# Gated state mixer: own buffers for the first triangular level, decay products split around the level updates, state values one level up, last turns inside the output tiles

## The reference, cut to what matters

```python
decay = jnp.exp(jnp.where(tril, gc[..., :, None] - gc[..., None, :], -jnp.inf))
k_beta = kc * bc
lmat = jnp.where(strict, jnp.einsum('bhnid,bhnjd->bhnij', k_beta, kc) * decay, 0.0)
rhs = jnp.concatenate([vc * bc, k_beta * jnp.exp(gc)[..., None]], axis=-1)
sol = lax.linalg.triangular_solve(lmat + jnp.eye(c), rhs, left_side=True, lower=True)
u, w = sol[..., :dv], sol[..., dv:]
attn = jnp.where(tril, jnp.einsum('bhnid,bhnjd->bhnij', qc, kc) * decay, 0.0)
...
def step(s, inp):                       # over the chunks, in order
    v_new = u_n - w_n @ s
    o = qd_n @ s + a_n @ v_new
    s = s * cd_n + kt_n.T @ v_new
    return s, o
```

## Time and profile before

| what | value |
|---|---|
| time before, median of 3 runs | 3153.77 us (3151.36 to 3159.57) |
| the profiled execution | 3158.95 us, its span 3157.2 us |
| TensorE busy / VectorE busy / ScalarE busy in the span | 96% / 68% / 50% |
| the stage | about 2046 to 2246 us of the span |

### The profile page before, as it was taken

How to read it: one execution, slowest core, us unless ns; L and a number is a source line. 1 busy time by engine, 2 the same in 40 slices (tenths; PEclk the granted TensorE clock), 3 DMA queues, 4 the chain that set the end, 5 groups by cost and what they waited for, 6 DMA issues and landing times.

```text
span 3157.2 us, 39144 instructions
## 1 busy us (share of the span) xinstructions
PE 3044.5 (96%) x14811; PEld 2349.9 (74%) x14811; DVE 2146.0 (68%) x2336; ACT 1593.9 (50%) x1907; POOL 371.9 (12%) x275
## 2 busy tenths in 40 slices
PE   8999899999999998999999989988999999999998
PEld 7667677777758766677777757877888888788887
DVE  3575888888863377788888865564577646767662
ACT  3573577777753373677777743342312214632211
POOL 0001122222220002122222130110000000000000
PEclk9999999999999999999999999999999999999999
DMA  7203899999962125899999943310232222232322
GB/s 279 109 1 133 300 359 363 357 361 362 362 249 80 37 78 218 318 359 359 362 368 362 358 134 94 74 33 1 94 107 81 94 107 94 88 113 86 101 94 80
DMA packets 174738, 600.50 MB, mean 190 GB/s; under 512 B 25537, under 2 KB 74865, under 8 KB 125203
## 3 DMA queue, kind: packets, MB, share of 16 engines
q1 hardware_dynamic: 140432, 541.22, 48.2%
q0 software_dynamic: 23680, 52.61, 4.7%
q10 hardware_dynamic: 10499, 4.91, 0.6%
HBM read 582.01 MB, written 48.23 MB: 200 GB/s over the span
## 4 chain that ended last, share of the span: by engine, by line
PE 87%; DVE 5%; ACT 3%; DMA 2%; issue 2%; POOL 0%; DVEq 0%; POOLq 0%; ACTq 0%
PE bank L1999 22%; PE bank L2001 22%; PE bank L2000 22%; PE bank L2011 3%; PE bank L2689 2%; PE bank L2389 2%; PE bank L2006 1%; PE bank L2063 1%; PE bank L2064 1%; PE bank L2007 1%; PE bank L2163 1%; PE bank L2430 1%; PE bank L2233 1%; PE bank L2183 1%; DMA ring<-w_gate 1%
## 5 line engine op out<-in xcount | busy, mean ns | idle before, releaser
L2000 PE MATMUL bank<-ring_rounded,big_rounded 128*96 128x512 f32 (+1 forms) x1768 | 695.8, 394 | 0.0
L3441 DVE TENSOR_TENSOR ring_rounded<-ring,big_rounded 128x2048 fp32r<-128x2048 f32 x252 | 572.2, 2289 | 69.8 <-ACT big_rounded L1408 68.5
L1408 ACT ACTIVATE big_rounded<-ring 128x2048 fp32r<-128x2048 f32 x252 | 479.5, 1916 | 69.9 <-DMA ring<-w_up 34.8
L2988 DVE TENSOR_TENSOR ring_rounded<-ring,ring_rounded 128x2048 fp32r<-128x2048 f32 (+2 forms) x118 | 260.3, 2246 | 333.9 <-ACT ring_rounded L1165 333.7
L1165 ACT ACTIVATE ring_rounded<-ring 128x2048 fp32r<-128x2048 f32 (+2 forms) x124 | 226.5, 1876 | 377.1 <-DMA ring<-ffn_w_down 152.7
L1999 PE MATMUL bank<-big_rounded 128*96 128x512 f32 x992 | 396.9, 400 | 9.1 <-DVE XH_rounded L3455 9.1
L2001 PE MATMUL bank<-big_rounded,XH_rounded 128*96 128x512 f32 x992 | 394.2, 397 | 0.0
L2000 PEld LDWEIGHTS bank<-ring_rounded,big_rounded 128*96 128x96 f32 (+1 forms) x1768 | 295.1, 167 | 110.3 <-issue 1.4
L3441 DVE TENSOR_TENSOR ring_rounded<-ring,ring_rounded 128x2048 fp32r<-128x2048 f32 x128 | 292.6, 2288 | 94.4 <-ACT ring_rounded L1408 94.1
L1408 ACT ACTIVATE ring_rounded<-ring 128x2048 fp32r<-128x2048 f32 x128 | 245.0, 1916 | 158.0 <-DMA ring<-w_gate 157.5
L1999 PE MATMUL bank<-ring_rounded,big_rounded 128*96 128x512 f32 (+1 forms) x776 | 309.8, 399 | 1.5 <-DVE big_rounded L4073 0.5
(11 more groups left out here) (486 smaller groups left out, 4844.2 us busy)
## 6 DMA issues: line engine op xcount, KB each, us to landing
ring<-w_up SPq DMA_DIRECT2D x128, 1024.0 KB, 7.7
ring<-w_down SPq DMA_DIRECT2D x128, 1024.0 KB, 6.6
ring<-w_gate SPq DMA_DIRECT2D x128, 1024.0 KB, 8.0
ring<-ffn_w_up SPq DMA_DIRECT2D x44, 1024.0 KB, 6.6
ring<-ret_gdn_w_in SPq DMA_DIRECT2D x8, 2048.0 KB, 12.7
ring<-ffn_w_down SPq DMA_DIRECT2D x8, 2048.0 KB, 7.7
expert_rows<-lnp POOLq DMA_DIRECT2D x1, 12288.0 KB, 40.4
ring<-odd_w_qkv SPq DMA_DIRECT2D x6, 2048.0 KB, 7.9
```

What stands on the lines that cost most here:

```text
L1408: act.activation(one_pass(expert_hi(j)), expert_raw(j), ACT.Copy).then_inc(signal("half_rounded").sem, 1)
L2000: pe.matmul(dst, x_hi, y_lo, start=False, stop=False)
L2988: dve.tensor_tensor(one_pass(w), w, parts(hi(c)[:, ks, :]), ALU.subtract).then_inc(split[c.pair], 1)
L3441: dve.tensor_tensor(one_pass(expert_raw(j)), expert_raw(j), parts(expert_hi(j)), ALU.subtract).then_inc(signal("half_split").sem, 1)
```

## The change

Five edits, all of them of order and of buffers. The number of products, transposes and VectorE instructions stays the same, and so do the transfers.

- ScalarE: `round_chunk` of chunk 7 moves from ahead of the work on chunk 6 to behind `gdn_rows(0)`. VectorE: the remainder of chunk 7 moves behind `gdn_exponents(1)`.
- Level 0 gets own buffers, `G["first"]`, which are the buffers of the mask and of the decay (`gm`, `dec`). Its masking is a function of its own, `first_weights`, and is done right behind `gdn_decayed`, before the end of chunk 7; `gdn_mask(2)` moves behind `first_level((0, 1))`. For the tiles (2, 3) the masking is done at level 4 of (0, 1), and the rest of level 0 stands ahead of `last_level((0, 1))` instead of behind it, in banks 4 and 5.
- `gdn_decayed` is split: `gdn_weighed` (three instructions that free the banks of kk and kq and write `LT`) stands between steps and updates of levels 2 and 4, the other three behind the updates.
- VectorE's `new_values` and `new_state` in the levels of (2, 3) stand one level earlier.
- `turn_y(2)` and `turn_y(3)` run between the halves of output tiles 1 and 2; `rest_of_y(2)` stands ahead of `y_out(3)`.

```diff
+        G["first"] = [G["gm"], G["dec"]]
@@ ScalarE
-                round_chunk(W["mix_in"][7])
                 for t in range(2):
                     keep(N_["GR"], 6, (2 * t,), ACT.Silu)
                     gdn_exps(t)
                     keep(N_["GR"], 6, (2 * t + 1,), ACT.Silu)
                     gdn_rows(t)
+                    if t == 0:
+                        round_chunk(W["mix_in"][7])
@@ TensorE
-                        turn_heads(u, G["T1"][t % 2])
+                        turn_heads(u, G["first"][t % 2])
...
+                first_level((2, 3))
                 last_level((0, 1))
-                first_level((2, 3))
...
-                mix_out(1, lambda: within(3))
-                turn_y(2)
-                mix_out(2)
-                turn_y(3)
+                def last_within():
+                    within(3)
+                    turn_y(2)
+
+                mix_out(1, last_within)
+                mix_out(2, lambda: turn_y(3))
                 mix_out(3)
@@ VectorE
+                def first_weights(ts):
+                    for t in ts:
+                        dve.tensor_tensor(G["first"][t % 2], G["LT"][t], rep(k("level0"), 1, GDN_HEADS), ALU.mult).then_inc(
+                            signal("first_level").sem, 1)
+                        dve.wait_ge(signal("first_level").sem, signal("first_level").next(dve))
...
                 gdn_exponents(0)
                 gdn_mask(1)
-                rest_of_chunk(W["mix_in"][7])
+                gdn_weighed(0)
                 gdn_decayed(0)
                 gdn_exponents(1)
-                gdn_mask(2)
+                rest_of_chunk(W["mix_in"][7])
+                gdn_weighed(1)
                 gdn_decayed(1)
+                first_weights((0, 1))
...
                 first_level((0, 1))
+                gdn_mask(2)
                 rest_of_T("yr_T")
                 for l in range(1, LEVELS - 1):
                     steps(l, (0, 1))
                     if l in (1, 3):
                         gdn_exponents(2 + l // 2)
+                    if l in (2, 4):
+                        gdn_weighed(1 + l // 2)
+                    updates(l, (0, 1))
                     if l == 2:
                         gdn_mask(3)
-                    updates(l, (0, 1))
-                    if l in (1, 3):
-                        gdn_decayed(2 + l // 2)
+                    if l in (2, 4):
+                        gdn_decayed(1 + l // 2)
+                    if l == 4:
+                        first_weights((2, 3))
+                first_level((2, 3))
...
                     steps(l, (2, 3))
+                    if l == 1:
+                        new_values(0)
                     if l == 2:
-                        new_values(0)
+                        new_state(0)
                     if l == 3:
-                        new_state(0)
+                        new_values(1)
                     if l == 4:
-                        new_values(1)
                         y_out(0)
-                    if l == 5:
                         new_state(1)
                     updates(l, (2, 3))
...
                 y_out(2)
+                rest_of_y(2)
                 y_out(3)
-                rest_of_y(2)
                 rest_of_y(3)
```

More of the change, by code:

```diff
@@ L480, in build @@
         for l in range(1, LEVELS):
+            if l == LEVELS - 1:
+                gdn_pick(2, turn0=4)
+                gdn_pick(3, turn0=5)
             level = level_uses(l, (0, 1))
@@ L491, in build @@
             next(level)
-        gdn_pick(2, turn0=0)
-        gdn_pick(3, turn0=1)
         for l in range(1, LEVELS):
@@ L3786, in gdn_exponents, with gdn_weighed @@
                     dve.wait_ge(signal("dec_raw").sem, signal("dec_raw").next(dve))
-                def gdn_decayed(t):
+                def gdn_weighed(t):
                     dve.wait_ge(signal("dec_exp").sem, signal("dec_exp").next(dve))
@@ L3800, in gdn_decayed @@
                     dve.wait_ge(drained[u.bank], u.n + 1)
+                def gdn_decayed(t):
+                    at = G["attnT"][t]
                     dve.tensor_tensor(at, at, rep(k("upto"), 1, GDN_HEADS), ALU.mult).then_inc(signal("attn_ready").sem, 1)
@@ L3806, in gdn_decayed @@
                     dve.wait_ge(dve_done.sem, dve_done.next(dve))
+                def first_weights(ts):
[3 more added lines that the diff above has]
+                        dve.wait_ge(signal("first_level").sem, signal("first_level").next(dve))
                 def first_level(ts):
                     for t in ts:
-                        dve.tensor_tensor(G["T1"][t % 2], G["LT"][t], rep(k("level0"), 1, GDN_HEADS), ALU.mult).then_inc(
-                            signal("first_level").sem, 1)
-                        dve.wait_ge(signal("first_level").sem, signal("first_level").next(dve))
-                        dve.tensor_tensor(G["InvT"][t], rep(ident, 1, GDN_HEADS), G["T1"][t % 2], ALU.subtract).then_inc(dve_done.sem, 1)
+                        dve.tensor_tensor(G["InvT"][t], rep(ident, 1, GDN_HEADS), G["first"][t % 2], ALU.subtract).then_inc(dve_done.sem, 1)
                         dve.wait_ge(dve_done.sem, dve_done.next(dve))
```

## The result

The changed kernel takes 3123.94 us (median of six runs, 3120.81 to 3130.17), the kernel before 3156.67 us in the same comparison (3151.36 to 3167.69). The ratio is 0.9894 with a 95% interval of 0.9882 to 0.9907: 1.06% faster, 33 us. The forecast was 3121.5 us in a range of 3112 to 3136.

The account below looks back on a forecast made before the run. The prediction took TensorE as the bound, full behind the stage, so its idle time in the stage was the budget. Six parts summed to 32.4 us, taken from the 3153.77 us median: 3121.4, stated as 3121.5, range 3112 to 3136.

Parts of the forecast that it names:

- Rivals 4 and 5: Whole kernel: 4, something behind takes it back, under 9.5 us, chance 0.03; 5, low clock through the levels, 3195, chance 0.02.
- A: Rounding of chunk 7: moved behind keep, it ends TensorE's 4.4 us wait and 1.6 us of low clock; 6.0 us.
- B: End of chunk 7 to level 1 of (0, 1): earlier masking shortens VectorE's work; 1.3 to 2.2 us, taken as 1.8.
- C: Levels 2 and 4 of (0, 1): split weights save 4.65 us each, less 1.2 us late in level 5; 8.1 us.
- D: Level 0 of (2, 3): no stop before the steps, 2.95 us, and steps at high clock, 2.2 us; 5.1 us.
- E: Levels 2 to 5 of (2, 3): state values one level earlier end TensorE's waits of 6.5 us; 6.2 us.
- F: Output tiles 2 and 3: turns between halves leave a wait of 0.5 us, then none; 5.2 us, low clock included.
- rival 3: Ahead of chunk 7: later rounding only moves the wait, so that part gives 1.5 us; 3125.9, chance 0.05.
- Rival 1: Transposes at both level 0 places: clock falls all the same, losing 2.2 and 1.8 us; 3125.4, chance 0.13.
- Rival 2: Levels of (2, 3): moved state instructions push updates back, so nothing is won there; 26.2 us saved, 3127.6, chance 0.07.

Follow-up runs that it names:

- again_1: The changed kernel, not edited, profiled a second time; its stage lasts 172.44 us against 173.49 in the first profile.
- again_2: The changed kernel, not edited, profiled a third time; its stage lasts 172.00 us against 173.49 in the first profile.
- u_round: Changed kernel with ScalarE's rounding of chunk 7 ahead of the work on chunk 6 again, VectorE's remainder earlier too; stage 5.7 us longer.
- u_weights: Changed kernel with gdn_weighed and gdn_decayed whole again behind the updates of levels 1 and 3; stage 8.05 us longer.
- u_state: Changed kernel with new_values and new_state of tiles (2, 3) one level later, as before; stage 6.6 us longer.
- u_turns: Changed kernel with turn_y(2) and turn_y(3) between output tiles again and rest_of_y(2) behind y_out(3); last section of the stage 3.85 us longer.
- order_2: Changed kernel with exponents of tiles 2 and 3 behind the updates of levels 1 and 3, gdn_decayed(3) behind level 0's transposes; stage 3.3 us shorter.
- order_4: order_2 with y_rounded(0) and rest_of_y(0) one level earlier; stage 4.0 us shorter than the changed kernel's, ratio to the kernel before 0.9869 to 0.9903.
- turns_in_5: Changed kernel with the eight transposes of level 0 of (2, 3) between steps and updates of level 5; stage 0.4 us shorter.
- order_3: order_2 together with the edit of turns_in_5; stage 3.2 us shorter than the changed kernel's.

## Why the prediction was right

The mechanism is the one forecast: TensorE's idle time was the budget, nothing behind the stage took it back, and no new wait over 1.1 us came up. Rivals 4 and 5, no effect and slower, fall with the measured time. By the forecast's own parts, predicted and measured in us:

```
part                        predicted   measured
A  round_chunk                 6.0        5.98
B  level 0 of (0, 1)           1.8        2.54
C  weights split               8.1        8.06
D  level 0 of (2, 3), order    2.95       3.08
   the same, clock             2.2        0.63   (again_1, again_2: 2.27)
E  state values                6.2        6.71
F  turns                       5.2        5.16
sum                           32.45      32.16
```

**A.** The rounding starts at 2057.59, which with the shift of 5.8 is 2063.4, as worked out; the remainder is done at 2064.1 (2069.9, forecast 2070). TensorE comes for the chunk at 2065.00, for its remainder at 2066.93, half by half. The first half was rounded at 2059.5 and its remainder done at 2061.9, so both have about 5 us to spare, more than the 1 to 3 forecast, and rival 3 did not happen. u_round undoes this part alone: 7.3 us in section I, of which 4.5 are the wait and the rest the clock. One reading of the earlier trace rows needs a word: the row of 2056.21 names a product of TensorE as what ended ScalarE's wait, but the load of chunk 7, for which `round_chunk` waits, landed only 0.4 us before it, at 2055.82, and the forecast's reading is the right one.

**B** was mis-sized by 0.7 us. The term took away half of a slowed instruction, 0.95 us, since GpSimd's last multiplication was to meet another VectorE instruction. GpSimd's timeline shows it, the last row here (the one of 1.29 us left out met no slowed neighbour):

```profile
2071.56 1.67 POOL L1114 TENSOR_TENSOR big<-big,bc 128x512 f32<-128x512 f32 x1 [24.68 <-ACT big L1678]
2076.95 3.23 POOL L1114 TENSOR_TENSOR big<-big,bc 128x512 f32<-128x512 f32 x1 [3.71 <-ACT big L1678]
...
2087.88 1.76 POOL L1114 TENSOR_TENSOR big<-big,bc 128x512 f32<-128x512 f32 x1 [4.15 <-ACT big L1678]
```

The last one runs beside L3825 and L3830, and both pairs took 1.41 to 1.42 us, their usual time. So the upper end of 2.2 was right. Another 0.3 came from the four remainders: 2.4 us to the next instruction, where 2.7 were put down. In the kernel before, the 16 transposes (L2869) ahead of them ran into a low clock, 3.07 us against 1.91 after (L2872); that this made the difference is not tested.

Why the last multiplication cost nothing shows when the pairs are taken apart:

```profile
2087.81 0.69 DVE L3825 TENSOR_TENSOR ring<-const,lnp 128x512 f32<-128x512 f32 x1
2088.54 0.69 DVE L3830 TENSOR_TENSOR ring<-const,bank 128x512 f32<-128x512 f32 x1
```

The second L3825 starts 0.07 us ahead of GpSimd's instruction and keeps its 0.69 us; the next ones, L3830, read a bank. In again_1 the distance is 0.07 us too. The Trainium skill (GPSIMD Engine Reference, Specifications) lists contention with VectorE instructions that have two SBUF inputs. The two stretched entries, L3978 and L2994 beside the first two rows, have two such inputs and agree; L3825 has them too and was not stretched, so the inputs alone don't decide, and the last section says what does here. B wasn't undone alone.

**C.** Level 2 lasts 8.36 us (forecast 8.4), level 4 8.71 (8.4), level 5 waits 1.04 (1.2). A wait of 1.1 in level 1 was not forecast. Of the 8.06, some 2 us are clock, which the forecast took in without naming it: before, from the products behind the two waits to the next steps were 4.54 and 4.32 us, against 3.44 at the full clock. u_weights brings 9.1 us back by itself, 1.0 more, because the fall behind its first wait lasted longer (3.78 us for the products that took 2.81 before).

**D.** The order gave its 3.08 us: `last_level` follows at 2129.93 and the steps at 2133.05 without a stop. The clock term failed in the profiled execution: the steps took 3.66 us instead of 2.05, so 0.63 of 2.2 came. It held in two of three executions of the same kernel. Over the nine profiles in which the same instructions stand there in the same order (the three, and u_round, u_weights, u_state, u_turns, order_2 and order_4) the clock fell in five: the term is worth 0.6 with the fall, 2.3 without, and some 1.4 in the mean. It is mis-sized, since the forecast took as nearly certain what is a chance. Rival 1, that the clock falls all the same, is thus true of this place in some executions and not in others; its other half is refuted, for B gave 2.54 us, and its 24 transposes in a row ran with a granted clock of 1.00 (the window 2087.00 to 2096.20), though they lasted only 2.6 us. The Trainium skill (TensorE: Matmul & The Clock Gate, the part on transposes) says that transpose mode doesn't count as TensorE being busy; this stretch doesn't show it, nor did the start of the program. D's order wasn't undone alone.

**E** was 0.5 us too small: the list of waits gave 6.5, of which 0.3 was taken off for level 3. The levels 2 to 5 of (2, 3) last 7.95, 7.60, 7.17 and 5.70 us, where before they lasted 9.79, 8.89, 8.89 and 7.56. Level 3 does gain least, 1.3, as the term had it, but levels 2 and 5 gain 1.84 and 1.86, more than their waits of 1.6. u_state brings the waits back one by one. Rival 2 is refuted by it.

**F.** Tile 2 starts at 2196.90 with a wait of 0.30 (forecast 0.5), tile 3 at 2202.96 without one. The second output chunk, named as the next that could be late, is rounded and has its remainder by 2207.9, and TensorE comes for it at 2208.40 without a wait. The sum is right, but its make-up was less certain than its text: 1.4 of it is a fall of the clock that u_turns did not have. That F and C came out to 0.1 us is therefore in part luck, since they hold falls that another execution may not have.

**The clock as a whole.** Before, the stage lost 11.9 us to it in six places (the sum of length times one minus granted clock); after, 1.7 in one. Part of each fall lies in a wait, where it costs nothing: by the parts the clock is some 6 of the 32.3 us (1.6 in A, 2.0 in C, 0.6 in D, 1.4 in F). The parts add up to 32.2 us, the stage to 32.3, the medians to 32.7, and 5.8 of the profiled spans' 38.2 are not the change's.

## What to carry to other kernels

In a stage where one engine idles and is full behind it, list its waits by the line that ends them, and for each ask which instructions stand ahead of that line on the late engine and whether they could stand behind: here five such moves, without one instruction less, won 1%. Behind a wait of 2 to 5 us add the clock that it may cost, up to 1.7 or 3.4 us, but as a chance: in one place a wait of 2.5 us had it in the kernel before and not in u_turns. And where an edit seems to make a fall of the clock vanish, profile the unedited kernel again before believing it; parts of a few us are to be measured between two fixed points of the trace, not by the whole time.

## What the runs showed of the hardware

Most of the clock's falls come in two sizes. At a granted clock of 0.57 over 4.00 us one loses 4.00 x 0.43 = 1.7 us, and the longer ones lose 3.4 (7.00 us at 0.53 in turns_in_5, and one such in each of u_weights and u_round). This is what TensorE loses if it never waits: the fall of 1.7 cost section V 1.6 us (37.13 against 35.50), but the same fall behind `last_level` of (2, 3) cost section VI only 0.6.

Over the whole program the span times one minus its mean granted clock is 46.4 us before and 32.1 after, and for the same changed kernel 26.0 in again_1 and 39.6 in again_2. The spans of the three executions of this kernel are 3119.0, 3113.5 and 3126.3 us; less these sums they are 3086.9, 3087.4 and 3086.7. So the clock explains nearly all of the 13 us between them. Of the 5.8 us by which the changed kernel was already ahead before the first edited line, it explains up to 3.4 (30.7 us up to there before, 27.3 after); the other 2.4 are no more than this stretch varies, clock taken out, between the three executions. The Trainium skill (TensorE: Matmul & The Clock Gate, the part on the clock gate) calls the number of slow products at the start run-variable; the three profiles agree, with 24, 24 and 21 products (transposes) 0.21 us apart before the pace doubles, and show it in the middle of a busy program as well.

What makes a fall stays open. The six before stand in or behind waits. The one that is left follows, in ten of twelve profiles, a `last_level`, whose products of 64 columns run without an idle gap, and no run took these products away. Transposes ahead of it aren't needed (order_3). Whether it comes, and behind which `last_level`, differs between executions of one program.

GpSimd's multiplications stretched VectorE's neighbours: a TENSOR_TENSOR of 512 columns from 0.69 to 1.67 us (L3978, 2072.12), and a pair of 2048 columns from 4.49 to 5.59 us (L2994, at 2076.72). Both lay under cover, so they cost nothing here. Who is hit follows from who began. In all five overlaps of the profiles before and after in which VectorE's instruction had two SBUF inputs, the one of VectorE that was under way when GpSimd's began kept its length, GpSimd's ended 1.1 to 1.2 us after it (1.67 to 3.33 us in all, 1.29 when alone). In the three in which another VectorE instruction with two SBUF inputs followed at once, that one was stretched past this end. One that read a bank (L3830) was not. So in these traces the two take turns by whole instructions, and a start 0.07 us earlier spared L3825.
